# A fused fp32 block on one core: biases ahead of the modulation, k tiles in the outer loop, the last unit of a stage bank by bank

## What is computed

```python
def ada_modulate(x, c, norm_g, ada_w, ada_b):
    ada = jax.nn.silu(c) @ ada_w + ada_b
    shift, scale, gate = jnp.split(ada, 3, axis=-1)
    h = rmsnorm(x, norm_g) * (1.0 + scale[:, None, :]) + shift[:, None, :]
    return h, gate[:, None, :]

def even_layer(...):
    h, gate_res = ada_modulate(x, c, norm_g, ada_w, ada_b)
    a, u, v, gate = _split(h @ in_w, EVEN_SIZES)
    ...
    return x + gate_res * (y @ out_w)
```

## Time and profile before

| | before |
|---|---|
| time, median of 3 runs | 1064.1 us (1063.83 to 1064.15) |
| profiled execution, time | 1064.55 us |
| profiled execution, span of the core | 1062.8 us |
| PE busy | 1011.3 us, 95% of the span |
| DVE busy | 723.7 us, 68% |
| ACT busy | 508.4 us, 48% |
| mean DMA rate | 207 GB/s |
| mean granted TensorE clock | 0.983 of full speed |
| chain that ended last, share on PE | 86% |

### The profile page before, as it was taken

One profiled execution on the slowest core, in us unless ns is written; L12 is line 12 of the kernel. 1 busy time (PEld: TensorE's weight loads), 2 busy tenths in 40 slices (PEclk: granted clock), 3 DMA queues, 4 the chain that ended last, 5 costly groups with the idle time before them and its releaser, 6 DMA issues.

```text
span 1062.8 us, 19611 instructions
## 1 busy us (share of the span) xinstructions
PE 1011.3 (95%) x8234; PEld 998.0 (94%) x8234; DVE 723.7 (68%) x1027; ACT 508.4 (48%) x740; POOL 41.6 (4%) x69
## 2 busy tenths in 40 slices
PE   6999999999999999998899999997997999999998
PEld 5899999989999999998899999997997989999998
DVE  4767967777673855767699878668786665556454
ACT  2554354456524454634555464454546444444442
POOL 2100000000000012401000000000000000000000
PEclk9999999999999999999899999998998999999999
DMA  9976576746772876468267776755433536656631
GB/s 356 364 257 238 183 254 238 260 164 212 237 245 73 303 252 210 159 248 277 73 239 286 262 247 226 253 199 169 143 106 101 158 103 216 199 198 196 211 110 41
DMA packets 138960, 219.58 MB, mean 207 GB/s; under 512 B 7161, under 2 KB 110922, under 8 KB 138872
## 3 DMA queue, kind: packets, MB, share of 16 engines
q1 hardware_dynamic: 136776, 214.00, 58.6%
q10 hardware_dynamic: 1136, 2.58, 0.7%
q0 software_dynamic: 960, 1.76, 0.6%
HBM read 217.25 MB, written 1.05 MB: 205 GB/s over the span
## 4 chain that ended last, share of the span: by engine, by line
PE 86%; DVE 7%; ACT 3%; issue 2%; DMA 2%; SPq 0%; ACTq 0%; DVEq 0%
PE pw L550 64%; PE pacc L550 22%; DVE WL L1505 1%; ACT AR L1074 1%; DMA ring<-in_even_in_w 1%; DVE hl L1606 1%; DVE SQT L1601 1%; DVE ACC L1521 1%; DMA AR<-in_cond 0%; ACT WH L1074 0%; ACT hh L1074 0%; PE pw L921 0%; PE pw L709 0%; SPq L311 0%; ACT YH L1074 0%
## 5 line engine op out<-in xcount | busy, mean ns | idle before, releaser
L1074 ACT ACTIVATE WH<-ring 128x1024 fp32r<-128x1024 f32 x288 | 302.2, 1055 | 293.6 <-PE pw L550 209.3
L550 PE MATMUL pw<-hh,WH 128*128 128x256 f32 x1408 | 404.8, 288 | 14.4 <-DVE MOD L1531 6.2
L1505 DVE TENSOR_TENSOR WL<-ring,WH 128x1024 fp32r<-128x1024 f32 x288 | 344.3, 1222 | 93.7 <-ACT WH L1074 93.2
L550 PE MATMUL pw<-hl,WH 128*128 128x256 f32 x1408 | 400.5, 284 | 0.0
L550 PE MATMUL pw<-hh,WL 128*128 128x256 f32 x1408 | 400.4, 284 | 0.0
L550 PEld LDWEIGHTS pw<-hh,WH 128*128 128x128 f32 x1408 | 272.2, 193 | 19.3 <-issue 8.8
L550 PEld LDWEIGHTS pw<-hl,WH 128*128 128x128 f32 x1408 | 272.2, 193 | 0.0
L550 PEld LDWEIGHTS pw<-hh,WL 128*128 128x128 f32 x1408 | 272.1, 193 | 0.0
L550 PE MATMUL pacc<-YH,WH 128*128 128x256 f32 x672 | 191.7, 285 | 3.5 <-issue 2.5
L550 PE MATMUL pacc<-YL,WH 128*128 128x256 f32 x672 | 190.1, 283 | 0.0
L550 PE MATMUL pacc<-YH,WL 128*128 128x256 f32 x672 | 190.1, 283 | 0.0
(11 more groups left out here) (245 smaller groups left out, 868.4 us busy)
## 6 DMA issues: line engine op xcount, KB each, us to landing
ring<-in_w_mod SPq DMA_DIRECT2D x72, 512.0 KB, 5.8
ring<-in_odd_in_w SPq DMA_DIRECT2D x56, 512.0 KB, 6.6
ring<-in_ada_w SPq DMA_DIRECT2D x48, 512.0 KB, 7.9
ring<-in_ffn_w_gate SPq DMA_DIRECT2D x44, 512.0 KB, 4.8
ring<-in_ffn_w_up SPq DMA_DIRECT2D x44, 512.0 KB, 5.5
ring<-in_ffn_w_down SPq DMA_DIRECT2D x44, 512.0 KB, 4.9
ring<-in_even_in_w SPq DMA_DIRECT2D x40, 512.0 KB, 6.6
ring<-in_even_out_w SPq DMA_DIRECT2D x16, 512.0 KB, 5.4
```

Of the source, the lines that this page charges most:

```text
L550: return eng.matmul(o, a, b, start=start, stop=stop, skip_group_check=True)
L1074: return eng.activation(dst, src, func, **kw)
L1505: tt(WL[:, i % NL, :], slot(half_of(i)), WH[:, i % NH, :].bitcast(F32), SUB).then_inc(s_lo, 1)
```

## The change

There are three edits. The first puts `ada("tail oo7")` and `ada("tail f1d10")` in the DVE program ahead of the modulation that follows. The second exchanges the loops over the k tile kk and the output half m in `cols_T`, `cols_N` and the gate and up units of `ffn`. The third lets a stage's last unit run over its four banks in the outer loop and its two pieces in the inner one, so that both pieces are counted as used only near its end; therefore ACT rounds the piece that needs the first of these buffers behind the squares (`cut_on`), and `pieces` skips it at its old place.

```diff
-                    for m in range(2):
-                        for kk in range(4):
+                    for kk in range(4):
+                        for m in range(2):
...
+                if tail is not None:
+                    W = [piece(2 * k + h, a) for h in range(2)]
+                    for q in range(4):
+                        for h in range(2):
+                            for n in (2 * q, 2 * q + 1):
+                                last = product(W[h], h, n)
+                            if h == 1 and q < 3:
+                                last.then_inc(s_acc, 1)
+                            elif q == 3:
+                                last.then_inc(s_use, 1)
+                        tail(q)
+                    return
...
                 for h in range(2):
-                    cut(2 * k + h)
+                    if h == 0 or name not in TAIL.values():
+                        cut(2 * k + h)
                     side.run(side.rate)
+
+            def cut_on(L):
+
+                cut(2 * index[TAIL[L]] + 1)
...
             squares(L_EVEN)
+            cut_on(L_EVEN)
             modulate(L_ODD, M1[:, 0:8])
...
             newton(d4, w4, t4)
+            ada("tail oo7")
             modulate(L_F1, M2[:, 0:8])
-            ada("tail oo7")
...
             norm(L_F1)
+            ada("tail f1d10")
             modulate(L_MIX, M2[:, 24:32])
-            ada("tail f1d10")
```

More of the change, by code:

```diff
@@ L636, in out_rows, with product @@
                 p.wait_ge(s_yl, i + 1)
+                def product(W, h, n):
+                    sl = slice(n * P, n * P + P)
+                    return mm3(pacc[:, n, :], (W[0][:, 0, sl], W[1][:, 0, sl]), (YH[:, i % 3, h, :], YL[:, i % 3, h, :]),
+                               first and h == 0 and n % 2 == 0, last_ and h == 1)
+                if tail is not None:
[10 more added lines that the diff above has]
+                    return
                 for h in range(2):
-                    H, Lo = piece(2 * k + h, a)
+                    W = piece(2 * k + h, a)
                     for n in range(8):
[L640 to L650, removed]
+                        last = product(W, h, n)
+                    last.then_inc(s_use, 1)
                     if mid is not None and h == 0:
@@ L1305, in _ @@
             squares(L_ODD)
+            cut_on(L_ODD)
             eng.preload_act_table_set("silu_and_others")
@@ L1398, in _ @@
             squares(L_F1)
+            cut_on(L_F1)
             side.flush()
@@ L1471, in _ @@
             squares(L_MIX)
+            cut_on(L_MIX)
             modulate(L_F2, M2[:, 48:56])
```

## The result

| | before | after |
|---|---|---|
| time, median of 4 runs | 1064.12 us (1063.83 to 1064.37) | 1045.90 us (1045.21 to 1048.63) |
| profiled execution, time and span | 1064.55, 1062.8 us | 1045.93, 1044.2 us |
| PE busy | 1011.3 us | 1004.2 us, 96% |
| DVE, ACT busy | 723.7, 508.4 us | 723.6, 507.6 us |
| mean granted TensorE clock | 0.983 | 0.995 |

The ratio of the times is 0.9834, with a 95% interval from 0.9816 to 0.9851: the change makes the kernel 1.5 to 1.8% faster. Forecast were 1047.1 us, in a range of 1044.0 to 1052.0.

A forecast was written before the change was run, and what follows sets the result against it. PE, busy for 95% of the span, was taken as the bound. Terms 0.6 + 2.3 + 8.1 + 6.2 + 0.75 - 0.3 - 0.7 = 17.0 us, taken from 1064.1, gave 1047.1 us; range 1044.0 to 1052.0.

The forecast's parts named there:

- L_F1: Start of stage L_F1: with the add ahead, unit f1u0 starts at 509.5 instead of 517.85, 8.35 us; net 8.1.
- L_MIX: Start of stage L_MIX: with the add ahead, unit wu1 starts at 742.0 instead of 748.23, 6.2 us, 1.4 of it low clock.
- I take 0.25 us more waiting than before: Third unit of L_F1: PE waits for DVE to read a bank, 0.25 us longer than the earlier 0.97 us.
- 0.3 us are the lower clock: Start of L_F1: of the 8.35 us, 0.3 come from the lower clock idle PE had fallen to, some 7 from the wait.
- L_ODD: First unit of L_ODD: qk0 ends at 232.6 instead of 234.91, 2.3 us with the clock high; 1.1 if it falls.
- L_EVEN's 0.6: First unit of L_EVEN: clock falls with either order; filling waits gains between nothing and 2.3 us, taken as 0.6.
- A: Rival: clock falls again in first units of L_ODD, L_MIX or both, costing 1.2 and 0.7 us; about 1050; chance 0.16.
- B: Rival: later in L_F1, DVE work that doesn't move up loses most of the 8.1 us; 1055; chance 0.07.
- C: Rival: PE's bank hangs on more than the add, so L_F1 and L_MIX still start behind the modulation; 1061.5; chance 0.03.
- D: Rival: changing output every three matmuls costs PE time; 14 ns each eat the 17 us, 20 ns give 1071; chance 0.02.
- E: Rival: changing banks makes PE pause until the clock falls inside units; near 1240 if all 44 gate and up units; chance 0.01.
- The case that the Trainium skill tells of: Cycling through PSUM banks left small idle times between groups and the clock went up and down; by it, a loss.

The follow-up runs named there:

- experiment 5: Kernel before, order kept, with 33 more warm matmuls behind spread r2 in L_F1 and 27 more behind the spread in L_MIX: 1060.48 us, ratio 0.9969.
- experiment 3: Kernel before with only the last units bank by bank, with the later WH piece: 1066.56 us, ratio 1.0019.
- experiment 1: Kernel before with only the two bias adds moved ahead of the modulation: 1051.26 us, ratio 0.9872 to the kernel before.
- 6: Kernel after, with DVE's second WL piece behind the x updates in the last units of L_ODD and L_F1: 1043.62 us, ratio 0.9807; run again, 1041.83 us.
- experiment 2: Kernel before with only k moved outside m, at the three places where the loops stand: 1059.72 us, ratio 0.9952.

## Why the prediction was right

**Edit 1.** Right in both its terms and in the path that it names: L_F1 gave 8.40 us (8.35), L_MIX 6.11 (6.2); the add is free, in DVE's idle time. Two sizes inside were wrong. Of "I take 0.25 us more waiting than before" 0.08 came. DVE's queue of WL pieces and x updates ended at 512.48 us, and ACT, which also had to read the bank, ended its first read at 512.43: DVE began its own at 512.46, with nothing to spare. And "0.3 us are the lower clock" in L_F1 was too small by far: experiment 5 shows 1.8 us behind the wait (in L_MIX 1.5, where 1.4 was said). The term stood nevertheless, since it was the distance between two starts, worked out from the last hl and the WL piece, and not a sum of wait and clock.

**Edit 2.** L_ODD 2.35 (2.3), L_F2 0.65 (0.75). The choice that the clock would stay high in L_ODD held in all nine profiles with k outside. That the loop order is the reason isn't shown: of the four profiles with m outside, two fell there (before and 3) and two did not (1 and 5). In 1 and 5 the first unit of L_ODD gained 1.3 us on before with the old loop order, by the clock alone; so of the 2.35 us only 1.0 is surely the exchange of the loops, and the rest was partly luck. L_EVEN's 0.6 was too small, and the step at fault is "its clock falls there with either order". With a fall the gain is 7.81 - 7.33 = 0.48 against the profile of before, near what I took (against the other profiles with m outside it is 0.7 to 1.2); without one it is 1.28. Both occur.

**Edit 3.** Right in sign, place and, in the profile, size: 0.27 and 0.71 us lost (0.3 and 0.7), for the first square behind a late DVE; no gain in any stage. That DVE's two WL pieces are the cause was shown by moving one of them (6). What the prediction lacked is that DVE's lateness varies: with a weight piece that landed late, L_ODD's tail cost 1.2 us in experiment 3.

**The sum.** In the order of the program: 0.13 + 1.28 + 2.35 - 0.27 + 8.40 - 0.72 + 6.11 + 0.65 = 17.9 us, against 16.95. The other 0.7 of the span's 18.6 is the shorter clock fall inside L_MIX (0.92 us), less 0.2 us, of which 0.08 is the third unit of L_F1 and the rest lies in places that I don't name. Of the sum's miss of 1.65 us, then, more than half is clock that falls where nothing was changed, and most of the rest is clock in L_EVEN.

**The rivals.** A, a fall in first units, didn't occur in L_ODD or L_MIX in any profile with both edits 1 and 2. B, the head start of L_F1 given back: the difference is 11.77 us at the third unit and 11.75 at the stage's 657.67 us mark, so nothing was lost. C falls with the first rows of the profile after and with experiment 1. D and E fall with experiment 2 and the 11.52 us of two column units. The case that the Trainium skill tells of and that I had weighed under E ("TensorE: Matmul & The Clock Gate", section "A second HAM failure mode: psum-queue depth-cycling") isn't repeated here: banks alternate every three matmuls, and the granted clock through 506 to 512 us is 1.00.

## What to carry to other kernels

When PE waits for a small write at a stage's start, look what stands ahead of that write in its engine's own queue; here 0.16 us of work, placed behind 7 us of modulation, held a PSUM bank and with it 13 us. A long idle time on a PE-bound kernel costs more than its length (7.1 and 1.8 us here), and what ends it should be judged with that in it. Getting PE to a point earlier is a loss if the engine that must answer it there isn't early too: first move the other engine's deferrable work behind the answer.

## What the runs showed of the hardware

The spread between executions of one kernel goes along with the clock. The four runs of 6 had mean granted clocks of 0.993, 0.995, 0.996 and 0.998, and took 1045.4, 1043.92, 1043.32 and 1041.84 us. The clock fell at a few places that came back in many kernels (near 38, 143, 456, 648 and 795 us, in the times of the faster kernels), in some executions and not in others. The two profiles of after fell at the same three places (142, 647 and 804 us) and had the same span of 1044.2 us. What decides in a single execution stays open. It means that a difference of under 2 us between two of these kernels can't be told from a handful of runs, while two traces compared matmul by matmul just ahead of a place and just behind it told 0.1 us; and that a term like the one of L_EVEN has more than one value.
